# First block of a three-layer trunk: scores of the first units inside the input chunks, fill steps in a table, output tile 0 between the last units

## What is computed

```python
mod   = split(silu(c) @ w_mod[i] + b_mod[i], 6)          # shifts, scales, gates: 6 sections of 1024
h, hc = rmsnorm(x) * (1 + sc1) + sh1, rmsnorm(ctx) * ...  # layer 0 keeps both streams, layer 1 only x
u     = h @ w_in                                          # ten groups of 256 columns
y_sc  = b_gate * conv3(c_gate * x_in)                     # short convolution
y_mla = softmax(q_mla k_mla^T) v                          # 4 heads, latent + context keys (512)
y_cf  = silu(layernorm(conv31(a * sigmoid(g)))) @ w_pw    # 31-tap depthwise convolution
y_na  = softmax(q k^T + bias/window) v                    # 4 heads, 512 keys
x     = x + gate1 * rmsnorm(concat(y_sc, y_mla, y_cf, y_na) @ w_out)
x     = x + gate2 * rmsnorm(relu(hm @ w1)**2 @ w2)
```

## Time and profile before

| | |
|---|---|
| median of 3 runs | 1616.68 us |
| the profiled execution | 1615.48 us, span 1613.6 us, mean granted clock 0.954 |
| PE busy | 1498.8 us (93%) |
| DVE, ACT, POOL busy | 914.4, 683.3, 76.0 us |
| input chunks, layer 0 and 1 (PE) | 43.9 to 171.6 us, 733.3 to 822.5 us |
| attention, layer 0 and 1 | 171.6 to 306.4 us, 822.5 to 906.0 us |
| output chunks begin | 306.4 us, 906.0 us |

### The profile page before, as it was taken

One profiled execution on the slowest core, in us unless ns is written; L12 is line 12 of the kernel. 1 busy time (PEld: TensorE's weight loads), 2 busy tenths in 40 slices (PEclk: granted clock), 3 DMA queues, 4 the chain that ended last, 5 costly groups with the idle time before them and its releaser, 6 DMA issues.

```text
span 1613.6 us, 23514 instructions
## 1 busy us (share of the span) xinstructions
PE 1498.8 (93%) x9372; PEld 1274.7 (79%) x9372; DVE 914.4 (57%) x1343; ACT 683.3 (42%) x1101; POOL 76.0 (5%) x95
## 2 busy tenths in 40 slices
PE   5999789889999999998988889998999999799997
PEld 3787556677888888878865679887999999698986
DVE  1677243454343332468933565556989555686866
ACT  3421344454132231454333474446444564564544
POOL 1300000000000000006500000000000000000000
PEclk8999789899999999998999989999899999899999
DMA  9421426421141322226347255445345434345442
GB/s 378 135 103 54 155 105 236 182 105 66 39 156 52 130 78 106 103 83 191 126 157 280 80 179 191 183 182 183 131 159 182 157 131 143 144 157 182 182 180 108
DMA packets 34337, 236.95 MB, mean 147 GB/s; under 512 B 4304, under 2 KB 4432, under 8 KB 6736
## 3 DMA queue, kind: packets, MB, share of 16 engines
q1 hardware_dynamic: 31936, 228.29, 38.5%
q0 software_dynamic: 2320, 7.51, 1.6%
HBM read 234.73 MB, written 2.00 MB: 147 GB/s over the span
## 4 chain that ended last, share of the span: by engine, by line
PE 81%; DVE 8%; ACT 5%; DMA 4%; issue 1%; SPq 0%; ACTq 0%; DVEq 0%
PE ps L493 43%; PE ps L531 22%; PE ps L509 4%; DMA w<-in_stream 3%; DVE w_lo L405 2%; PE ps L730 2%; PE ps L588 2%; DVE tiny L1785 1%; PE ps L763 1%; DMA C<-in_consts 1%; ACT U L1280 1%; DVE U L1678 1%; PE ps L735 1%; PE ps L593 1%; PE ps L627 1%
## 5 line engine op out<-in xcount | busy, mean ns | idle before, releaser
L493 PE MATMUL ps<-h_hi,w_hi 128*128 128x256 f32 (+1 forms) x1600 | 510.3, 319 | 6.0 <-DVE h_lo L1556 4.6
L493 PE MATMUL ps<-h_lo,w_hi 128*128 128x256 f32 (+1 forms) x1600 | 505.6, 316 | 0.0
L493 PE MATMUL ps<-h_hi,w_lo 128*128 128x256 f32 (+1 forms) x1600 | 505.3, 316 | 0.0
L395 ACT ACTIVATE w_hi<-w 128x1024 fp32r<-128x1024 f32 x332 | 331.6, 1053 | 253.6 <-DMA w<-in_stream 253.6
L405 DVE TENSOR_TENSOR w_lo<-w,w_hi 128x1024 fp32r<-128x1024 f32 x332 | 393.0, 1227 | 67.1 <-ACT w_hi L395 65.4
L493 PEld LDWEIGHTS ps<-h_hi,w_hi 128*128 128x128 f32 x1600 | 311.8, 195 | 28.3 <-issue 8.1
L493 PEld LDWEIGHTS ps<-h_lo,w_hi 128*128 128x128 f32 x1600 | 311.7, 195 | 17.6 <-issue 0.5
L493 PEld LDWEIGHTS ps<-h_hi,w_lo 128*128 128x128 f32 x1600 | 311.3, 195 | 17.4
L531 PE MATMUL ps<-w_hi,g_hi 128*128 128x512 f32 x472 | 187.9, 398 | 3.9 <-DVE g_lo L2056 3.6
L531 PE MATMUL ps<-w_lo,g_hi 128*128 128x512 f32 x472 | 187.0, 396 | 0.0
L531 PE MATMUL ps<-w_hi,g_lo 128*128 128x512 f32 x472 | 187.0, 396 | 0.0
(11 more groups left out here) (246 smaller groups left out, 1690.0 us busy)
## 6 DMA issues: line engine op xcount, KB each, us to landing
w<-in_stream SPq DMA_DIRECT2D x214, 1024.0 KB, 4.8
U<-rpb_rows POOLq DMA_DIRECT2D x32, 64.0 KB, 2.3
SW<-in_small POOLq DMA_DIRECT2D x2, 896.0 KB, 6.6
X<-in_x SPq DMA_DIRECT2D x1, 1024.0 KB, 13.0
X<-in_ctx SPq DMA_DIRECT2D x1, 1024.0 KB, 15.1
X<-in_masks POOLq DMA_DIRECT2D x1, 1024.0 KB, 5.0
GA<-in_gpost POOLq DMA_DIRECT2D x2, 512.0 KB, 4.5
out<-X SPq DMA_DIRECT2D x2, 512.0 KB, 2.6
```

The lines of the kernel that those rows point to most:

```text
L395: act.activation(k.w_hi[:, c.slot, half], k.w[:, c.slot, half], ACT.Copy).then_inc(k.hi_done, 1)
L493: last = pe.matmul(k.banks(2 * c.pair, n, j * (512 if tiles == 2 else n)), w[a][:, c.slot, at:at + 128], h[b][:, kt * stride:kt * stride + n],
```

## The change

- The first two units' `scores` move into the input chunks: `scores(0)` after `nq`, `scores(1)` in the middle of `nv`; their maxima and exponentials, and `probabilities(0)`, stand with the `nq` chunk on DVE and ACT, so before those engines read `nv`. The MLA's small products all stand one chunk earlier, `latent_squares` in the middle of `sc_x`.
- PSUM banks are renumbered: scores use 4 to 7, transposes 0 and 1, outputs 2, fill steps 3.
- The fill steps stand in a table of three slots per iteration in place of `fill_at`; ACT reads slot 0's step ahead of `exps`. The order of units is by query tile, MLA first.
- Mean and variance of the layer norm come from DVE's `bn_stats`, `bn_aggr`; four squares and four sums on ACT go.
- The output weights are split by ACT and DVE half by half inside the last iterations. PE begins output tile 0 before the last unit is through: `transposes` of the last unit and `values` of the last two stand inside that tile's second half. Tile 0's products use banks 4 and 5.
- The tap counts are redistributed, and `pool_tables` waits for the end of layer 1's input chunks.

```diff
-FILL_LEAD = 4
-FILL_REST = 5
-def fill_at(l, slot, units):
-    total, slots = FILL_TO[l] - FILL_FROM[l], 2 * units + FILL_LEAD - FILL_REST
-    return [FILL_FROM[l] + n for n in range(total) if n * slots // total == slot + FILL_LEAD]
+def fill_table(l):
...
+        return [([rows(2, 0)], [rows(2, 1)], []),
+                ([cf("cf_t", 0)], [feats(2)], []),
...
-TAPS = (0, 9, 9, 9, 9, 7, 7, 8, 4, 0), (0, 14, 7, 7, 7, 5, 10, 6, 6, 0)
+TAPS = (0, 10, 9, 9, 9, 8, 3, 9, 5, 0), (0, 15, 6, 6, 3, 2, 9, 6, 15, 0)
+TAPS_FIRST = 5
...
 def unit_banks(k, c, tiles, t, half):
 
+    if KINDS[c.first] == "out" and t == 0:
+        return k.banks(4 + half, 512)
...
-    pairs = [("mla", 0, 512, 2), ("na", 0, 512, 6)] + ([("mla", 256, 256, 2), ("na", 256, 256, 6)] if l == 0 else [])
-    return [(kind, pair, qt, q0, nk, kt0) for kind, q0, nk, kt0 in pairs for pair in range(2) for qt in range(2)]
+    stages = [("mla", 0, 512, 2), ("mla", 256, 256, 2), ("na", 0, 512, 6), ("na", 256, 256, 6)]
+    return [(kind, pair, qt, q0, nk, kt0) for kind, q0, nk, kt0 in stages if l == 0 or q0 == 0
+            for qt in range(2) for pair in range(2)]
+def out_feeds(l, units):
+    if l == 0:
+        return {(units - 4, "middle"): (0, 0), (units - 4, "end"): (0, 1), (units - 3, "middle"): (1, 0),
+                (units - 3, "end"): (1, 1)}
+    return {(units - 3, "middle"): (0, 0), (units - 3, "end"): (0, 1)}
...
 (pe_mixers)
-    between = {4: latent_squares, 5: latent_rows, 6: rotary_and_keys, 7: queries_and_values, 8: rotary_queries}
+    middle = {4: latent_squares, 9: lambda: scores(1)}
+    after = {4: latent_rows, 5: rotary_and_keys, 6: queries_and_values, 7: rotary_queries, 8: lambda: scores(0)}
...
-    for i in pipeline(units):
-        if i + 2 < len(units):
-            scores(i + 2)
-        for n in fill_at(l, 2 * i, len(units)):
-            pe_mod_step(k, pe, n, 7)
-        if 0 <= i < len(units):
-            transposes(i)
-        for n in fill_at(l, 2 * i + 1, len(units)):
-            pe_mod_step(k, pe, n, 7)
-        if i >= 1:
-            values(i - 1)
-    k.wait(pe, "o_lo", l, len(units) // 2)
+    for i in range(end - 2):
+        scores(i + 2)
+        if i == 0:
+            for reads, count in ((k.act_read, ACT_READ_COUNT), (k.dve_read, DVE_READ_COUNT)):
+                pe.wait_ge(reads, count[c0 + 9])
+        fill(i, 0)
+        transposes(i)
+        fill(i, 1)
+        if i >= 1:
+            values(i - 1)
+        fill(i, 2)
+    transposes(end - 2)
+    values(end - 3)
+    def mixed(t):
+        return lambda: k.wait(pe, "o_lo", l, end // 2 - (4 if l == 0 else 2) + t + 1)
...
+    before = {(t, 0, 6): mixed(t) for t in range(tiles)}
+    before.update({(0, 0, 4): convolved, (0, 1, 0): lambda: transposes(end - 1), (0, 1, 2): lambda: values(end - 2),
+                   (0, 1, 4): lambda: values(end - 1)})
...
 (act_cf_statistics)
-    for t in range(tiles):
-        o.link(act.activation(k.SW[:, 0:256], k.cft[:, t * 256:t * 256 + 256], ACT.Square,
-                              bias=k.tiny[:, CF_NEG + t:CF_NEG + t + 1],
-                              accum_out=k.tiny[:, CF_VAR + t:CF_VAR + t + 1]))
+    k.wait(act, "cf_var", l, CF_HALVES[l])
...
 (dve_mod_step)
-        dve.tensor_scalar(k.tiny[:, CF_NEG:CF_NEG + tiles], k.tiny[:, CF_SUM:CF_SUM + tiles], -1.0 / 256, None,
-                          ALU.mult).then_inc(k.s("cf_neg"), 1)
+            o.link(dve.bn_stats(parts, k.cft[:, tile * 256:tile * 256 + 256]))
+            last = dve.bn_aggr(k.tiny[:, CF_MEAN_VAR + 2 * tile:CF_MEAN_VAR + 2 * tile + 2], parts)
...
 (act_mixers, the loop over the ten input chunks)
+        elif kind == "nq":
+            k.wait(act, "cf_conv", l, 1)
+            exps(0)
+            exps(1)
...
-        if i + 2 < len(units):
-            exps(i + 2)
-        for n in fill_at(l, 2 * i, len(units)):
-            act_mod_step(k, act, n, 7, o)
+        fill(i, 0)
+        exps(i + 2)
+        transposed(i)
+        feed((i, "middle"))
+        fill(i, 1)
+        if i >= 1 and units[i - 1][1] == 1:
+            outputs(i - 1)
+        fill(i, 2)
+        feed((i, "end"))
...
 (dve_mixers, the loop over the ten input chunks)
-        if kind == "sc_x":
+        if kind == "q":
+            conv_taps(TAPS_FIRST)
             k.wait(dve, "latent_std", l, 1)
...
+        if kind == "nq":
+            maxima(0)
+            maxima(1)
+            probabilities(0)
...
 (pool_program)
+            pool.wait_ge(k.chunk_mm, FIRST["win", 1] + len(WIN))
             pool_tables(k, pool, o)
```

More of the change, by code:

```diff
@@ L756, in values @@
         k.wait(pe, "pt_dve", l, i + 1)
-        if qt == 0 and i >= 2:
+        if pair == 0 and i >= 2:
             k.wait(pe, "o_lo", l, i // 2)
@@ L1039, in act_mod_step @@
         act.wait_ge(k.s("mod_mm"), mod_mm_count(n + 1))
-        for t in range(2):
-            tile = 2 * part + t
-            last = act.activation(k.cft[:, tile * 256:tile * 256 + 256], k.banks(bank, 256, t * 256), ACT.Copy,
-                                  accum_out=k.tiny[:, CF_SUM + tile:CF_SUM + tile + 1])
-        last.then_inc(k.s("mod_read"), 1)
+        act.activation(k.cft[:, part * 512:part * 512 + 512], k.banks(bank, 512),
+                       ACT.Copy).then_inc(k.s("mod_read"), 1)
     elif kind == "cf_b":
@@ L1220, in act_mixers, with exps @@
     eps = k.C[:, C_EPS:C_EPS + 1]
+    units = attention_units(l)
+    def exps(i):
+        nk = units[i][4]
+        k.wait(act, "nmax", l, i + 1)
+        if i >= 3:
+            k.wait(act, "pt_mm", l, i - 2)
+        for e in range(2):
+            nmax, total = 16 + 2 * (i % 2) + e, 20 + 2 * (i % 3) + e
+            last = act.activation(b["p"][i % 3][:, e * nk:e * nk + nk], k.banks(4 + 2 * (i % 2) + e, nk), ACT.Exp,
+                                  bias=k.tiny[:, nmax:nmax + 1], accum_out=k.tiny[:, total:total + 1])
+        last.then_inc(k.s("exp"), 1)
     for j, kind in enumerate(WIN):
@@ L1268, in act_mixers, with transposed @@
     k.wait(act, "sc_y", l, 2)
[L1269 to L1273 removed]
+    def transposed(i):
         nk = units[i][4]
[L1275 to L1282 removed]
@@ L1284, in act_mixers @@
[L1284 to L1304 removed]
+        k.wait(act, "pt_mm", l, i + 1)
@@ new lines, in fill, with feed @@
+    def fill(i, slot):
+        for n in FILL[l][i][slot]:
+            act_mod_step(k, act, n, 3)
+    end = len(units)
+    out = At(FIRST["out", l])
+    feeds = out_feeds(l, end)
+    def feed(at):
+        if at in feeds:
+            feed_hi(k, act, out + feeds[at][0], feeds[at][1:])
+    for i in range(end - 2):
+        fill(i, 0)
[7 more added lines that the diff above has]
+        feed((i, "end"))
@@ L1307, in act_mlp @@
+    transposed(end - 2)
+    if l == 1:
+        feed_hi(k, act, out + 1, (0,))
+    outputs(end - 3)
+    if l == 1:
+        feed_hi(k, act, out + 1, (1,))
+    act_feed_rest(k, act, out)
+    transposed(end - 1)
+    outputs(end - 1)
 def act_mlp(k, act, o, l):
@@ L1737, in between, with maxima, probabilities @@
             rotate(b["qr"][:, 0:256], k.banks(7, 256))
+    units = attention_units(l)
+    def maxima(i):
+        kind, pair, qt, q0, nk, _ = units[i]
+        k.wait(dve, "scores", l, i + 1)
+        sc2 = k.ps[:, 4 + 2 * (i % 2):6 + 2 * (i % 2), :]
+        if kind == "na" and q0 == 0:
+            bias = b["bias"].rearrange("p (h q n) -> p h q n", h=HEADS, q=2)[:, 2 * pair:2 * pair + 2, qt, :]
+            o.link(dve.tensor_tensor(sc2[:, :, 0:256], sc2[:, :, 0:256], bias, ALU.add))
+        dve.tensor_reduce(k.tiny[:, 16 + 2 * (i % 2):18 + 2 * (i % 2)], sc2[:, :, 0:nk], AX.X, ALU.max,
+                          negate=True).then_inc(k.s("nmax"), 1)
+    def probabilities(i):
+        nk = units[i][4]
+        k.wait(dve, "exp", l, i + 1)
+        rc = k.tiny[:, 26 + 2 * (i % 2):28 + 2 * (i % 2)]
+        o.link(dve.reciprocal(rc, k.tiny[:, 20 + 2 * (i % 3):22 + 2 * (i % 3)]))
+        for e in range(2):
+            p = b["p"][i % 3][:, e * nk:e * nk + nk]
+            last = dve.tensor_scalar(p, p, rc[:, e:e + 1], None, ALU.mult)
+        last.then_inc(k.s("p"), 1)
     for j, kind in enumerate(WIN):
@@ new lines, in fill, with feed @@
+    def fill(i, slot):
+        for n in FILL[l][i][slot]:
+            dve_mod_step(k, dve, n, 3, o)
+    end = len(units)
+    out = At(FIRST["out", l])
+    feeds = out_feeds(l, end)
+    def feed(at):
+        if at in feeds:
+            feed_lo(k, dve, out + feeds[at][0], feeds[at][1:])
+    for i in range(end - 2):
+        maxima(i + 2)
+        fill(i, 0)
+        probabilities(i + 1)
+        transposed(i)
+        feed((i, "middle"))
+        fill(i, 1)
+        if i >= 1 and units[i - 1][1] == 1:
+            outputs(i - 1)
+        fill(i, 2)
+        feed((i, "end"))
@@ L1824, in dve_down @@
+    probabilities(end - 1)
+    transposed(end - 2)
+    if l == 1:
+        feed_lo(k, dve, out + 1, (0,))
+    outputs(end - 3)
+    if l == 1:
+        feed_lo(k, dve, out + 1, (1,))
+    dve_feed_rest(k, dve, out)
```

(2 more changed lines are left out.)

267 lines of the change are left out of this document (127 added, 140 removed).

## The result

| | before | changed |
|---|---|---|
| median of 6 runs (lowest to highest) | 1618.39 us (1611.22 to 1619.35) | **1552.60 us** (1552.26 to 1554.15) |
| ratio, 95% interval | 1 | 0.9603 (0.9586 to 0.9620) |
| span of the profiled execution | 1613.6 us | 1550.8 us |
| mean granted clock over the span | 0.954 | 0.971 |

The kernel is 65.8 us faster; in the profiled executions the span is 62.8 us shorter.

A forecast was written before the change was run, and what follows sets the result against it. PE was taken to bound the kernel: 70.6 us of idle time and low clock could go, 24.3 us of waits and clock would be left, so 1616.7 - 46.3 = 1570.4 us, range 1554 to 1590 us.

The forecast's parts named there:

- What bounds the kernel: PE in both layers' attention and output tile 0: idle time and low clock, 70.6 us that could go.
- The waits that remain: PE's waits left in both attention loops, from a walk on paper: 6 us in each layer, plus 2 us.
- the 2 us of friction: Latencies that a walk on paper through both attention loops leaves out, put at 2 us.
- The clock: Low-clock stretches of PE in the two layers' attention: six kept, 1.6 us each, 9.6 us still lost.
- Added waits: Layer 1's sc_x: PE's wait for ACT's square becomes 1.7 us, 0.7 more; tables beside the attention cost 0.
- The first unit's chain: Start of attention: maxima, table load and exponentials move beside nv products, removing PE's 2.79 us wait.
- The waits between fill steps: Attention loops: reading slot 0 first and spacing fill steps removes waits of 1.14, 3.9 and 5.2 us.
- The end: End of attention: waits of 3.14, 0.93 and 1.5 us go into tile 0; 0.7 us late in layer 0.
- rival 1: Clock stays high and waits hide better: 6 us left in all, gain 64, 1552 to 1558 us; 12%.
- Rival 2: Waits come back elsewhere: 28 of 44 us stay idle, 15 us of clock, gain 27, about 1589 us; 18%.
- Rivals 3 and 4: Slower, clock locks low, 1680 us, 3%; or no change, loads or DVE pace both attention loops, 2%.
- Rival 3: PE's attention mixture holds the low level throughout: 152 us of work take up to 136 us more, 1680; 3%.

The follow-up runs named there:

- features_twice: Changed kernel, but each of the ten features steps in the attention stretches issues its two-column products twice: 1594.20 us.
- even_fill: Changed kernel, but its fill steps stand in the old order, spread evenly over two slots an iteration, in place of the table: 1578.65 us.
- act_late: Changed kernel, but ACT runs the exponentials of unit i + 2 ahead of its read of slot 0, as before: 1578.44 us.
- tables_early: Changed kernel, but POOL makes the rope tables beside layer 1's input chunks, as before, not behind the last of them: 1559.81 us.
- start_outside: Changed kernel, but units 0 and 1 are scored behind nv, their maxima, exponentials and first probabilities after the readers of nv: 1552.86 us.
- the filled tails: Changed kernel, but PE fills its waits before the last tile's transposes with unused wide products: 12 a wait, 1563.32 us; 7 a wait, 1547.08 us.
- read_waits: Changed kernel, but PE waits after each of its 51 fill steps until ACT or DVE has read the bank: 1603.74 us.
- even_act_late: Changed kernel with both the old, evenly spread fill order and ACT's exponentials ahead of its read of slot 0: 1591.91 us.

## Why the prediction was right, and where it was too small

The direction held, and most of the parts that it named; the time came out below the range, since one term of the sum was too large.

**What bounds the kernel** was right: nearly all that the change gave came from PE's idle time and clock in the two attentions.

**The waits that remain** were named one by one, and most came as named: after cf_b 0.6 and 1.1, measured 1.8 together; after cf_pw 0.5, 0.9 and 1.3, measured 0.5, 1.0 and 1.3; the first iterations of layer 1 0.8 and 1.1, measured 0.7 and 1.0; two gates in one slot 0.7, measured 0.7. Too dear were the weight halves (1.0 and 1.5, measured 0.5 at most and 0.9), the last copy in tile 0 (0.7, measured none) and the 2 us of friction. The sum of 14 us measured 9.5.

**The clock** is the step that failed, the 9.6 us of low level kept in the sum. "I keep six such, 9.6 us: features steps stream two columns and stay." Two low stretches were left in the attentions, 211.6 to 215.0 and 819.2 to 822.6, some 3.4 us of lost time. The kind of step was rightly suspected, as features_twice shows, but of the ten single features steps of 1.9 us, with wider work between, only two stood ahead of a low stretch. What kept the level down before was, I take it, that they met with pauses: even_fill and act_late bring 21 us of idle time each and clocks of 0.89 to 0.94. No run takes the two apart. The sum also held no clock outside the attentions. The input chunks of the kernel before had a low stretch each that the changed kernel does not have, 104.2 to 107.6 and 773.2 to 776.6 us (clock 0.50), both behind the MLA's one-column products (L662, L666), the first with PE busy for all of the 7.1 us ahead. So the chunks grew by 3.0 and 1.8 us where their added scores alone are 8 x 1.06 = 8.5 us and `sc_x` takes off 0.3: 3.3 us better. The start was 1.7 us better, which is chance (below). So, against a forecast of 46.3: 4.5 for the waits, 6.2 for the clock in the attentions, 3.3 for that in the chunks, 1.7 for the start and 1.0 for `sc_x` make 63.0; the 62.8 measured fit that, as all the rest of the kernel is 0.5 us longer. The signs say the same: attention with tile 0 was to take about 112 and 78 us with six low stretches or so, and took 106.6 and 71.7 with two.

**Added waits.** The wait ahead of the `sc_x` squares was forecast at 1.7 us, 0.7 more than before; it is 0.72. That it would be about 4 us if DVE came no sooner is what tables_early measured, 3.9. The walk's price of a tap was too low, though: over layer 1's chunks the 60 taps kept DVE busy for 28.8 us, 0.48 each and not 0.41. bn_stats with its aggregate takes 0.41 + 0.18 = 0.59 us a tile, against 0.7 taken, on an engine that has the time:

```profile
L1681 DVE BATCH_NORM_STATS2 tiny<-hs x4: 394/411/428, 183.2 to 189.3; 128x6 f32<-128x256 f32 x4
L1682 DVE BATCH_NORM_AGGREGATE tiny<-tiny x4: 182/182/182, 183.7 to 189.7; 128x2 f32<-128x6 f32 x4
```

**The first unit's chain** was credited with the 2.79 and 0.83 us of the earlier trace rows. The time went, but not by that part: start_outside has the scores back behind `nv` and loses nothing. The 2.79 us was a wait for ACT's read of a "rows" step (L1037 in the earlier trace rows); ACT's new order is what removes such waits, and act_late, with the scores still moved, brings back 1.05 us at that place. **The waits between fill steps** had the right causes, table and ACT's order, each worth 26 us when the other stays and 39 together. **The end** was right, and larger than its idle time by the clock.

**The rivals.** The measured time is that of rival 1, "the clock stays high and waits hide better" (1552 to 1558 us, 12%), and the clocks of 0.98 are its mark, though 9.5 us stayed idle where it had 6 us left in all. Its ground, a simple reading of the Trainium skill (TensorE: Matmul & The Clock Gate, Part 1, What's actually happening) by which activity releases the clock, only goes half way: the filled tails and read_waits agree with it, while in features_twice PE was idle for 2.9 of 85.5 us and had a clock of 0.88, so being busy did not by itself keep the level up. Rival 2 (1589) did not come, though it is nearly what even_act_late makes. Rivals 3 and 4 are out: the clock never locked, and at 247 and 250 GB/s the loads kept up. (Rival 3's price was short: 152 us of work at full clock take up to 152 us more at half the clock, not 136.)

**What stays open.** Whether the clock term can be foreseen to better than a few us was not settled: low stretches shift from run to run. Undoing start, end, and fill with ACT's order, one by one, gives 0 + 17 + 39 = 56 of the 65.8 us, though parts undone singly need not add up; the tables' 7 us are a wait that the earlier squares would have brought, not one of the kernel before. What the rest belongs to (the squares on DVE, the order of units) was not tried by itself.

## What to carry to other kernels

Count what a wait costs on TensorE twice: the wait, and the low clock behind it, which here added 21 us to 27 us of idle time. When one bank or one slow reader carries the side work, let the reader serve it ahead of work that waits for a third engine, and put other products between two such steps; that gained more here than starting the first unit earlier, which gained nothing. Where a wait of some us on TensorE can't be removed, try wide products into a bank that is about to be overwritten, sized by a measured product to end before the wait does; at five waits of 6 us they gained 5.5 us here.
